# Two recurrent branches and one linear-attention block in fp32: 64-row products on four array tiles, the order of the last gated-delta steps, and the order and shape of two small products in the opening

## The reference

```python
def step(s, inp):                       # s: one 64x64 state per head and direction
    w_c, u0_c, p_c, qg_c, kd_c, ge_c = inp
    u = u0_c - jnp.einsum('nhcd,nhde->nhce', w_c, s)
    o = jnp.einsum('nhcd,nhde->nhce', qg_c, s) + jnp.einsum('nhij,nhje->nhie', p_c, u)
    s = ge_c[..., None, None] * s + jnp.einsum('nhcd,nhce->nhde', kd_c, u)
    return s, o
```

```python
w_log = -softplus(-(w0 + einsum('bld,edc->eblc', tanh(wd), w2))) - 0.5     # decay, e: direction
a = sigmoid(a0 + einsum('bld,edc->eblc', ad, a2))                          # rate
...
s = s * w_t + (s @ -kk_t) * b_t + v_t * k_t;  y = s @ r_t
...
bonus = jnp.sum(r_h * k_bonus * r_k, axis=-1, keepdims=True) * v_h
```

## Time and profile before

| | us |
|---|---|
| median of 3 runs (3910.45 to 3918.28) | 3911.17 |
| the profiled execution | 3914.69 |
| its span in the trace | 3912.9 |

### The profile page before, as it was taken

The page is one execution under the profiler, slowest core; times in us unless marked ns, Lnnn a source line. Parts: engine busy times, 40 slices in busy tenths (PEclk is TensorE's granted clock), DMA queues, the critical chain, the costliest instruction groups (busy, mean ns, idle before and its releaser), DMA issues. The chain is left out here.

```text
span 3912.9 us, 62415 instructions
## 1 busy us (share of the span) xinstructions
PE 3585.2 (92%) x26072; PEld 2205.3 (56%) x26072; DVE 2247.0 (57%) x3955; ACT 1250.2 (32%) x2191; POOL 283.2 (7%) x233
## 2 busy tenths in 40 slices
PE   7789989979999979897988999899999997999999
PEld 4367436666654457544775654466666665444443
DVE  3476467746663467357665665266666667433453
ACT  3253353334531244254524443112222122231001
POOL 0011100000000011000000000122222221000000
PEclk9899998979999989998988999999999998999999
DMA  4334112120042233302112013211111101312231
GB/s 156 100 87 135 54 33 81 60 103 13 15 161 98 81 112 97 102 22 79 49 51 102 13 67 112 67 39 44 44 39 44 44 28 57 110 48 86 90 108 45
DMA packets 301831, 281.29 MB, mean 72 GB/s; under 512 B 18016, under 2 KB 274144, under 8 KB 301552
## 3 DMA queue, kind: packets, MB, share of 16 engines
q1 hardware_dynamic: 301552, 277.30, 21.9%
HBM read 203.93 MB, written 73.33 MB: 71 GB/s over the span
## 5 line engine op out<-in xcount | busy, mean ns | idle before, releaser
L3390 DVE SCALAR_TENSOR_TENSOR cv<-glu,params,cv 128x1024 f32<-128x1024 f32 x240 | 361.0, 1504 | 6.4
L1474 PE MATMUL ps<-hT,w_cols 128*128 128x512 f32 x576 | 254.3, 601 | 13.5 <-PEq L158 13.5
L399 PE MATMUL ps<-hT,w_cols 128*128 128x512 f32 x448 | 203.5, 615 | 3.3 <-PEq L158 3.3
L1474 PEld LDWEIGHTS ps<-hT,w_cols 128*128 128x128 f32 x576 | 110.8, 193 | 152.2 <-issue 150.3
L3686 PE MATMUL ps<-hT,wr 128*128 128x512 f32 x360 | 161.7, 592 | 0.0
L399 PEld LDWEIGHTS ps<-hT,w_cols 128*128 128x128 f32 x448 | 87.7, 197 | 116.0 <-issue 116.0
L3366 POOL TENSOR_TENSOR Sp<-Sp,Rp 128x520 f32<-128x520 f32 (+1 forms) x56 | 88.6, 1581 | 565.4 <-DVE W L3407 565.4
L3149 PE MATMUL ps<-hT,w_f 128*128 128x347 f32 x384 | 116.8, 464 | 7.4 <-DMA w_f<-in_w_in 7.4
L3164 PE MATMUL ps<-w_i,hT 128*128 128x128 f32 x1024 | 120.7, 277 | 0.0
L3164 PEld LDWEIGHTS ps<-w_i,hT 128*128 128x128 f32 x1024 | 116.1, 192 | 2.2 <-issue 1.6
L3686 PEld LDWEIGHTS ps<-hT,wr 128*128 128x128 f32 x360 | 68.4, 190 | 86.1 <-issue 86.1
(11 more groups left out here) (929 smaller groups left out, 7253.6 us busy)
## 6 DMA issues: line engine op xcount, KB each, us to landing
w_cols<-in_w_in SPq DMA_DIRECT2D x32, 512.0 KB, 3.8
wr<-in_w_in SPq DMA_DIRECT2D x24, 512.0 KB, 5.1
hT_hbm<-hT SPq DMA_DIRECT2D x2, 4096.0 KB, 14.1
hT<-hT_hbm SPq DMA_DIRECT2D x2, 4096.0 KB, 15.4
fh<-hT_hbm SPq DMA_DIRECT2D x16, 512.0 KB, 4.5
fh_again<-hT_hbm SPq DMA_DIRECT2D x16, 512.0 KB, 4.5
x<-in_x SPq DMA_DIRECT2D x8, 512.0 KB, 8.2
ahead<-kb_hbm SPq DMA_DIRECT2D x16, 256.0 KB, 3.4
```

The costliest lines, as they stand in the source:

```text
L399: q = pe.matmul(ps[:, proj_bank(n, b), :], lhsT=wc[:, n % 3, k, :], rhs=hT[:, k, P + b * 512:P + (b + 1) * 512], start=(k == 0), stop=(k = ...
L1474: q = pe.matmul(ps[:, proj_bank(n, b), :], lhsT=wc[:, n % 3, k, :], rhs=hT[:, k, P + b * 512:P + (b + 1) * 512], start=(k == 0), stop=(k = ...
L3390: vec.scalar_tensor_tensor(out=cv[:, h % 2, :], in0=src, scalar=w, in1=cv[:, h % 2, :], op0=ALU.mult, op1=ALU.add).then_inc(*VEC(f"tap{h}_ ...
```

## The change

Four edits, in both layers.

1. **64x128 products as pairs of 64x64 ones.** L904 and L969 (RWKV), L1754, L1765 and L1824 (gated delta): the stationary operand is cut into LOW and HIGH columns, two instructions in place of one, written to partitions 0 to 63 and 64 to 127 of the same bank.
2. **The last four gated-delta steps in another order**, on TensorE and on VectorE.
3. **Low-rank products** issued as decay, rate, decay, rate in place of decay, decay, rate, rate; each `low_rank(n)` waits for both results of the one before at its start; and the four stand between halves of `project(2)` and `project(3)`.
4. **Bonus sums** with 32 stationary columns each, written to four column groups of the array: 64 instructions for 16.

The diff, with part of the indentation taken off:

```diff
@@ -385,10 +385,10 @@
         q = pe.matmul(ps[:, narrow_bank(t), 0:TM_NOW], lhsT=hT[:, k, (t + 1) * P:(t + 2) * P], rhs=wt[:, k, :], start=(k == 0), stop=(k == KD - 1))
     q.then_inc(*PE(f"tm{t}"))
 
-def project(n):
+def project(n, halves=(0, 1)):
     if L == 0 or n >= 3:
         pe.wait_ge(*DMA[f"w{n}"])
-    for b in range(2):
+    for b in halves:
         if n == 0 and L == 0:
             pe.wait_ge(*VEC[f"h{NT - 1}_{b}"])
         elif n == 1 and L == 0:
@@ -407,15 +407,14 @@
         pe.wait_ge(*ACT["tanh"])
     else:
         pe.wait_ge(*ACT[f"dec{n - 1}"])
-    for b in range(2):
-        q = pe.matmul(ps[:, 4 + b, :], lhsT=w2a2[0:64, e, m * P:(m + 1) * P], rhs=th[:, half(b)], start=True, stop=True)
-    q.then_inc(*PE(f"dec{n}"))
-    if n:
         pe.wait_ge(*ACT[f"rate{n - 1}"])
     for b in range(2):
-        q = pe.matmul(ps[:, 6 + b, :], lhsT=w2a2[64:128, e, m * P:(m + 1) * P], rhs=rw[64:128, LOWRANK, half(b)],
+        d = pe.matmul(ps[:, 4 + b, :], lhsT=w2a2[0:64, e, m * P:(m + 1) * P], rhs=th[:, half(b)], start=True, stop=True)
+        if b == 1:
+            d.then_inc(*PE(f"dec{n}"))
+        r = pe.matmul(ps[:, 6 + b, :], lhsT=w2a2[64:128, e, m * P:(m + 1) * P], rhs=rw[64:128, LOWRANK, half(b)],
                       start=True, stop=True)
-    q.then_inc(*PE(f"rate{n}"))
+    r.then_inc(*PE(f"rate{n}"))
 
 def square_sums(m):
     pe.wait_ge(*VEC[f"sq{m}"])
@@ -430,8 +429,9 @@
     pe.wait_ge(*ACT["kk_ln1"])
     for t in range(NT):
         for m in range(2):
-            q = pe.matmul(ps[:, 4, 4 * t + 2 * m:4 * t + 2 * m + 2], lhsT=bonus[:, m, t * P:(t + 1) * P], rhs=cst("sel"),
-                          start=True, stop=True)
+            for j in range(0, P, 32):
+                q = pe.matmul(ps[j:j + 32, 4, 4 * t + 2 * m:4 * t + 2 * m + 2], lhsT=bonus[:, m, t * P + j:t * P + j + 32],
+                              rhs=cst("sel"), start=True, stop=True)
     q.then_inc(*PE("bonus"))
 
 def turn_values(m, bank, t0, t1):
@@ -450,11 +450,13 @@
 project(0)
 project(1)
 low_rank(0)
+project(2, [0])
 low_rank(1)
-project(2)
+project(2, [1])
 low_rank(2)
+project(3, [0])
 low_rank(3)
-project(3)
+project(3, [1])
 square_sums(0)
 project(4)
 square_sums(1)
@@ -901,8 +903,9 @@
         for em in range(4):
             for h in range(2):
                 c0 = slice(64 * h, 64 * h + 64)
-                q = pe.matmul(ps[:, RB + h, RD * em:RD * em + RD], lhsT=KR[c0, s % 5, em, 0, :], rhs=Zc[c0, s % 2, em, :], start=False,
-                              stop=False, skip_group_check=True)
+                for t in (LOW, HIGH):
+                    q = pe.matmul(ps[t, RB + h, RD * em:RD * em + RD], lhsT=KR[c0, s % 5, em, 0, t], rhs=Zc[c0, s % 2, em, :],
+                                  start=False, stop=False, skip_group_check=True)
         q.then_inc(*PE(f"R{s}"))
 
     def first_half(s):
@@ -966,8 +969,9 @@
         for em in range(4):
             for h in range(2):
                 c0 = slice(64 * h, 64 * h + 64)
-                pe.matmul(ps[:, b + h, RD * em:RD * em + RD], lhsT=KR[c0, s % 5, em, 1, :], rhs=Zc[c0, s % 2, em, :], start=(em == 0),
-                          stop=False, skip_group_check=True)
+                for t in (LOW, HIGH):
+                    pe.matmul(ps[t, b + h, RD * em:RD * em + RD], lhsT=KR[c0, s % 5, em, 1, t], rhs=Zc[c0, s % 2, em, :],
+                              start=(em == 0), stop=False, skip_group_check=True)
         for em in range(4):
             for h in range(2):
                 for t in (LOW, HIGH):
@@ -1751,8 +1755,10 @@
             e, m = em // 3, em % 3
             for h in range(2):
                 c0 = slice(64 * h, 64 * h + 64)
-                pe.matmul(ps[:, RB + h, GD * em:GD * em + GD], lhsT=gq[c0, 6 + m, tok(s, e)], rhs=cst("nident")[c0, c0], start=(em == 0),
-                          stop=False, skip_group_check=True)
+                for t in (0, 64):
+                    here = slice(tok(s, e).start + t, tok(s, e).start + t + 64)
+                    pe.matmul(ps[t:t + 64, RB + h, GD * em:GD * em + GD], lhsT=gq[c0, 6 + m, here], rhs=cst("nident")[c0, c0],
+                              start=(em == 0), stop=False, skip_group_check=True)
 
     def keys_on_state(s):
         pe.wait_ge(*VEC[f"KQ{s}"])
@@ -1762,8 +1768,9 @@
             e, m = em // 3, em % 3
             for h in range(2):
                 c0 = slice(64 * h, 64 * h + 64)
-                q = pe.matmul(ps[:, RB + h, GD * em:GD * em + GD], lhsT=KQ[c0, s % 2, e, 3 + m, :], rhs=S[c0, s % 2, em, :], start=False,
-                              stop=False, skip_group_check=True)
+                for t in (LOW, HIGH):
+                    q = pe.matmul(ps[t, RB + h, GD * em:GD * em + GD], lhsT=KQ[c0, s % 2, e, 3 + m, t], rhs=S[c0, s % 2, em, :],
+                                  start=False, stop=False, skip_group_check=True)
         q.then_inc(*PE(f"R{s}"))
 
     def first_half(s):
@@ -1821,8 +1828,9 @@
             e, m = em // 3, em % 3
             for h in range(2):
                 c0 = slice(64 * h, 64 * h + 64)
-                pe.matmul(ps[:, b + h, GD * em:GD * em + GD], lhsT=KQ[c0, s % 2, e, m, :], rhs=S[c0, s % 2, em, :], start=(em == 0),
-                          stop=False, skip_group_check=True)
+                for t in (LOW, HIGH):
+                    pe.matmul(ps[t, b + h, GD * em:GD * em + GD], lhsT=KQ[c0, s % 2, e, m, t], rhs=S[c0, s % 2, em, :],
+                              start=(em == 0), stop=False, skip_group_check=True)
 
     def out_of_chunk(s):
         b = pair_of_banks(f"o{s}")
@@ -1894,16 +1902,16 @@
         keys_on_state(s)
         if s < NT - 1:
             decays(s + 1)
+        first_half(s)
         keys(s)
+        across(s)
         pairs(s, 0, 0)
-        first_half(s)
+        second_half(s)
         pairs(s, 1, 0)
-        across(s)
         out_of_state(s)
-        second_half(s)
+        to_state(s)
         if s < NT - 1:
             values_in(s + 1)
-        to_state(s)
         out_of_chunk(s)
 
 @block.scalar
@@ -2192,14 +2200,14 @@
     for s in range(4, NT):
         right_side(s)
         old_state(s)
+        first_half(s)
+        keys(s)
+        across(s)
+        query_pairs(s, 0)
+        second_half(s)
+        query_pairs(s, 1)
         if s < NT - 1:
             decays(s + 1)
-        keys(s)
-        query_pairs(s, 0)
-        first_half(s)
-        query_pairs(s, 1)
-        across(s)
-        second_half(s)
         new_state(s)
         if s == 4:
             rest_of_own(1)
```

## The result

The changed kernel takes 3852.35 us (median of 4 runs, 3846.05 to 3852.55) where the kernel before takes 3911.19 (median of 4 runs beside them): ratio 0.9849, 95% interval 0.9834 to 0.9863. It is 59 us faster; the forecast had 85 and 3826. A later profile of the same kernel (label a_again, 3851.18 us) lies near the median and is used beside it.

What follows compares the result with a forecast made beforehand. TensorE, busy 92% of the span, was taken as the bound, through its time and gaps. Gains of 8.0 + 51.2 + 14.6 + 6.3 + 5.0 = 85 us from 3911.17 gave 3826 us, range 3806 to 3858.

Steps and rivals of the forecast that it cites:

- the first two rivals: 64x64 passes run two tiles at a time, 3849 us, chance 0.14; clock still falls in last gated-delta steps, 3851, chance 0.12.
- 64x64 products, what they hold TensorE: Four tiles run together: 48 gated-delta passes take 0.86 us for 1.49, an RWKV group 0.62 for 1.04.
- two tiles at a time: Rival for the 64x64 products: each pass keeps 0.031 us whatever runs beside it; 23 us lost, 3849 us, chance 0.14.
- tiles one at a time: Slower rival for the 64x64 products: tiles exclude each other, a pass takes 72 ns; 3966 us, chance 0.03.
- RWKV, 8.0 us: Shorter products in ten RWKV groups a layer, steps 4 to 7 mainly, gain 4.0 us a layer, 8.0 in all.
- The new order and the products in the gated delta: Last four gated-delta steps: waits covered, groups 0.63 us shorter, a step 11.7 us; with step 0's 1.3, gain 51.2 us.
- The clock: Gated-delta steps 4 to 6: TensorE nearly always busy, so five slow steps keep 2.4 GHz, 4.55 us each.
- Low-rank products and halves: Opening: low-rank products between projection halves take 17.6 us, against 20.10 or 24.70; gain 14.6 us, alternating by itself worth nothing.
- Bonus sums: Opening: group 1.3 us for 4.61, gain 6.3 us over both layers; clock staying up behind it, 5.0 us.
- Other engines: Rival: another engine takes over, VectorE in the new order or the opening; 3840 us, chance 0.08.
- the opening: Low-rank and bonus-sum stretches with their projections: forecast gain 15.2 us in layer 0 and 10.7 in layer 1.

Runs made afterwards that it cites:

- the opening alone: Kernel before with only the opening's two edits (projection halves between alternating low-rank products, bonus sums on four column groups): 3893.34 us, ratio 0.9952.
- the burst of layer 0: Changed kernel with the out_of_state group of gated-delta step 5 issued eight times over in both layers, here layer 0's: 3864.38 us in one run.
- products alone: Kernel before with only the five kinds of products as 64x64 pairs, old order and old opening: 3878.60 us, ratio 0.9917.

## Why the prediction was right or wrong

The total alone decides little: 3852 lies nearer to the first two rivals, 3849 and 3851, than to 3826, and within the range only because it is wide. The traces decide against both rivals; what the sum lacks lies elsewhere.

- **64x64 products, what they hold TensorE:** right. 0.86 and 0.62 us as taken; two tiles at a time and tiles one at a time both fall.
- **RWKV, 8.0 us:** the step that failed. The gain is there (0.7 to 1.0 us a step in steps 4 and 5), but it was put down as clear because "groups stand back to back" and the rest "lies in front of waits on ScalarE": only engines were counted as what can be late. TensorE's own instructions are. Both layers together have stops of 10.8 us against 1.6 before, and stretches at 1.2 GHz behind some of them. Measured -4.3 and -7.4 us for the two profiles in place of +8.0 (the opening alone already costs this stage 3.3 in layer 0), and kernels without this part are not slower.
- **The new order and the products in the gated delta:** the sizes were right, 11.53 us a step for 11.7, and no wait on VectorE left in steps 5 and 6 of layer 0. Over both stages 47.4 and 48.5 us against 51.2. Steps 4 to 6 give 47.1 and 47.3 of it, where the sum had 45.5. What lacks is in the last steps and in steps 0 to 3 of layer 1, where `join` now stops twice and stopped once before.
- **The clock:** the outcome was right (no slow step left), the reason was too narrow. It was put on the stretch with the two waits; either edit alone cures it, one with the waits in place. For what decides it the prediction had no measured rule, and none came out of the runs, so this part was right with some luck.
- **Low-rank products and halves:** right, 17.96 us for 17.6, and alternating at nothing.
- **Bonus sums:** right in place, 1.18 for 1.3 us and a projection of 13.84 for 13.8, over the 4.61 and 15.95 before; in the total it can't be seen, since the kernel with the old sums has fewer stops in `join` and in RWKV. The 128 passes start within 1.07 us, 8.4 ns each. The Trainium skill's rule of some 60 cycles a pass (TensorEngine Tiling (Array Packing), Instruction Overhead) would give an estimated 3.2 us, and its least time of 25 ns between starts (TensorE: Matmul & The Clock Gate, Wait — 56ns, not 53.3ns?) as much; the trace agrees with neither.
- **Other engines:** none took over; the sequencer's supply did, and no rival had it.

Of the 85 us forecast, a_again's trace shows 63.6, and the trace before lies 3.5 above its median, which leaves 60 (59 by the medians). Of the 21.4 that lack there, RWKV has 15.4, the opening 3.3, the gated delta 2.6, and the untouched stages 0.2.

## What to carry to other kernels

Splitting a pass into tiles doubles the instructions as well as halving the time: count instructions per microsecond, and compare with one packet each 3.6 us of quiet queues, less when they carry loads. Split where TensorE's time is bare and the queues are quiet; where large loads run, look for "issue" waits in the middle of a group, and for the instruction queue's packets beside them. Before adding up parts that each "save the clock", run them alone: a stretch at the lower level can be cured only once. And before crediting a change of a few us to an edit, compare the stages that it doesn't touch: an edit that changes the number of instructions can move, add or remove stops in all code behind it, at some 3 us each in `join` here.

## What was not expected of the hardware

- TensorE's instructions arrive in packets of 16 KB, one each 3.6 us on average while TensorE stands waiting for them in the burst of layer 0 (3.4 to 3.8). With the queues full of data for the last 7 us before it, one came only as the data ran out (13.5 us after the last one), and TensorE stood still for up to 2.9 us.
- 336 more passes of 64x64 in a quiet stretch cost 0.030 us each, twice what 48 cost in a row (0.71 us from the first to the last start, 0.0148 each): a short group is faster than a long one.
- The clock stayed at its upper level in six steps of six with TensorE idle 16% of a step (products alone), and in one of six with the same waits, 14% of the step, and longer groups between them (before); in two of six in another trace of the same code (the opening alone).
